# Four norms between dense stages taken in two halves of 256 tokens, with the last product unit ahead and the first one behind computed half by half

## What is computed

```python
def rms_norm(x, g): return x * rsqrt(mean(x * x, axis=-1) + EPS) * g
def modulate(h, shift, scale): return h * (1 + scale) + shift

h = modulate(rms_norm(x, norm_g), shift, scale)     # one norm ahead of every stage
x = x + 0.5 * gate * swiglu(h, w_in, w_out)         # a stage reads h and adds to x
```

## Time and profile before

| | |
|---|---|
| runs | 2886.98, 2891.97, 2892.22 us; median 2891.97 |
| profiled execution | 2890.92 us, of which the core's span is 2889.1 |
| granted TensorE clock, mean | 0.978 of full speed |
| PE (TensorE matmul) busy | 2775.0 us, 96% of the span |
| PEld (weight load) busy | 2322.7 us, 80% |
| DVE (VectorE) busy | 1519.1 us, 53% |
| ACT (ScalarE) busy | 835.0 us, 29% |
| chain that ended last | PE 93%, DVE 5%, ACT 1%, issue 1%, DMA 1% |

### The profile page before, as it was taken

One profiled execution on the slowest core, in us unless ns is written; L12 is line 12 of the kernel. 1 busy time (PEld: TensorE's weight loads), 2 busy tenths in 40 slices (PEclk: granted clock), 3 DMA queues, 4 the chain that ended last, 5 costly groups with the idle time before them and its releaser, 6 DMA issues.

```text
span 2889.1 us, 33968 instructions
## 1 busy us (share of the span) xinstructions
PE 2775.0 (96%) x13286; PEld 2322.7 (80%) x13286; DVE 1519.1 (53%) x2054; ACT 835.0 (29%) x913; POOL 75.6 (3%) x151
## 2 busy tenths in 40 slices
PE   4999998999999999999999999999999999999999
PEld 3888876888878888788788887898898878778887
DVE  6735544735556367544563455657565533354343
ACT  3212232212231122321321423345545422222221
POOL 0000000000001000000000000000000000000000
PEclk9999997999999999999999999999999999999999
DMA  7634521635526355232363332111111342222322
GB/s 272 227 130 168 196 84 67 230 117 186 176 93 235 126 170 196 88 102 98 104 228 111 128 99 92 56 37 52 45 46 43 109 153 89 87 88 87 102 90 85
DMA packets 92932, 353.43 MB, mean 122 GB/s; under 512 B 10528, under 2 KB 11296, under 8 KB 84000
## 3 DMA queue, kind: packets, MB, share of 16 engines
q1 hardware_dynamic: 73120, 250.05, 25.9%
q0 software_dynamic: 19280, 101.23, 9.6%
q10 hardware_dynamic: 432, 0.75, 0.1%
HBM read 343.60 MB, written 8.39 MB: 122 GB/s over the span
## 4 chain that ended last, share of the span: by engine, by line
PE 93%; DVE 5%; ACT 1%; issue 1%; DMA 1%; SPq 0%; DVEq 0%; ACTq 0%
PE ps L1682 24%; PE ps L1684 24%; PE ps L1683 24%; PE ps L1818 4%; PE ps L1820 4%; PE ps L1819 4%; PE ps L2060 1%; PE ps L2054 1%; PE ps L2008 1%; DVE w_raw_lo L971 1%; DVE h_lo L1107 1%; DVE ada_first L976 0%; PE ps L1767 0%; PE ps L1701 0%; PE ps L1913 0%
## 5 line engine op out<-in xcount | busy, mean ns | idle before, releaser
L1682 PE MATMUL ps<-h_hi,w_hi 128*128 128x512 f32 x2016 | 792.6, 393 | 19.6 <-DVE h_lo L1107 15.9
L1684 PE MATMUL ps<-h_hi,w_lo 128*128 128x512 f32 x2016 | 790.3, 392 | 0.0
L1683 PE MATMUL ps<-h_lo,w_hi 128*128 128x512 f32 x2016 | 790.3, 392 | 0.0
L581 ACT CAST w_hi<-w_raw 128x2048 fp32r<-128x2048 f32 (+1 forms) x240 | 422.1, 1759 | 622.6 <-PE ps L1684 537.0
L971 DVE TENSOR_TENSOR w_lo<-w_raw,w_hi 128x2048 fp32r<-128x2048 f32 (+1 forms) x219 | 458.5, 2094 | 127.8 <-ACT w_hi L581 127.3
L1682 PEld LDWEIGHTS ps<-h_hi,w_hi 128*128 128x128 f32 x2016 | 382.6, 190 | 109.1 <-issue 27.9
L1683 PEld LDWEIGHTS ps<-h_lo,w_hi 128*128 128x128 f32 x2016 | 382.8, 190 | 80.1
L1684 PEld LDWEIGHTS ps<-h_hi,w_lo 128*128 128x128 f32 x2016 | 382.0, 189 | 80.2
L1682 PE MATMUL ps<-g_hi,w_hi 128*128 128x512 f32 x960 | 373.5, 389 | 0.0
L1684 PE MATMUL ps<-g_hi,w_lo 128*128 128x512 f32 x960 | 373.4, 389 | 0.0
L1683 PE MATMUL ps<-g_lo,w_hi 128*128 128x512 f32 x960 | 373.4, 389 | 0.0
(11 more groups left out here) (292 smaller groups left out, 2761.5 us busy)
## 6 DMA issues: line engine op xcount, KB each, us to landing
w_raw<-in_units SPq DMA_DIRECT2D x350, 512.0 KB, 4.5
ada<-in_ada_t POOLq DMA_DIRECT2D x56, 1024.0 KB, 6.5
w_raw<-in_units SPq DMA_DIRECT2D x128, 352.0 KB, 3.7
ada<-in_ada_t POOLq DMA_DIRECT2D x64, 512.0 KB, 5.0
ada_first<-in_ada_t SPq DMA_DIRECT2D x8, 1024.0 KB, 18.0
x_res<-in_x SPq DMA_DIRECT2D x4, 512.0 KB, 7.8
x_home<-x_res POOLq DMA_DIRECT2D x1, 2048.0 KB, 8.5
attn_home<-attn_out POOLq DMA_DIRECT2D x8, 256.0 KB, 2.3
```

The lines of the kernel that those rows point to most:

```text
L581: nc.scalar.copy(W_HI[u.slot][:, 0:n], W_RAW[u.slot][:, 0:n]).then_inc(hi_done, 1)
L1682: pe.matmul(dst, hi[:, k, c], rhs_hi(k), start=(k == 0), stop=False)
L1683: pe.matmul(dst, hi[:, k, c], rhs_lo(k), start=False, stop=False)
L1684: last = pe.matmul(dst, lo[:, k, c], rhs_hi(k), start=False, stop=(k == kt - 1))
```

## The change

Norms 3, 4, 5 and 7 are done for tokens 0 to 255 and then for 256 to 511 (`HALF[0]`, `HALF[1]`). `LATE[r]` are the tiles of X that the last unit finishes.

- TensorE, `last_unit`: the last unit ahead is computed for the first half of the tokens, then for the second (into other PSUM banks), with matmuls of 256 columns and each weight tile loaded for each half. The one-column sums of the first half stand ahead of the last three tiles of the second half. The spread of the first half's scale stands behind the unit.
- TensorE, `first_unit`: the first unit behind is likewise two passes over its eight tiles. The second half's sums stand behind tile 1 of the first pass, its spread behind tile 6.
- VectorE and ScalarE, `norm_halves` and `first_half`: the add to X, the late squares, the root, the diagonal, and the scale, shift and low-part steps are all done on 256 columns, twice.
- The late squares are no longer added to SSQ, but summed by TensorE with one-column matmuls of their own.
- In the last unit ahead, ScalarE's early squares and VectorE's sums stand ahead of the split of the next weights where they stood behind it (VectorE for all four, ScalarE for 3 and 4).
- `split_hi(ahead)` stands between the two halves on ScalarE, `split_lo(ahead)` near the end of the second half on VectorE.
- The MLP's first quarter is written out, and the loop of three quarters is one of two; three semaphores of the convolution become one.

```diff
+        LATE = {3: (7,), 4: (7,), 5: (6, 7), 7: (6, 7)}
...
+            def norm_halves(r, g, unit, ahead):
...
+                nc.scalar.activation(RSTD4[:, 16:17], EPS_C[:], ACT.Sqrt)
+                late(0)
+                half_root(0)
+                hi(0, 0)
+                hi(0, 1)
+                late(1)
+                hi(0, 2)
+                half_root(1)
+                hi(0, 3)
...
+                hi(0, 7)
+                if ahead is not None:
+                    split_hi(at(ahead))
+                for k in range(KD):
+                    hi(1, k)
...
+            def first_half(r, u, gate):
+
+                dve.wait_ge(half_done, N_BASE[r] - r + 1)
+                for n, k in enumerate(LATE[r]):
+                    last = add_half(0, k, BANK[2 * (u % 2) + n], gate)
+                last.then_inc(half_x, 1)
...
+                diagonal(0)
+                dve.wait_ge(mod_done, g + 1)
+                scaled(0, 0)
+                scaled(0, 1)
+                lo(0, 0)
+                second_half()
+                for k in range(2, 5):
+                    scaled(0, k)
+                    lo(0, k - 1)
+                diagonal(1)
+                for k in range(5, KD):
+                    scaled(0, k)
+                    lo(0, k - 1)
+                lo(0, KD - 1)
+                scaled(1, 0)
+                for k in range(1, KD):
+                    scaled(1, k)
+                    lo(1, k - 1)
+                    if ahead is not None and k == 6:
+                        split_lo(at(ahead))
+                lo(1, KD - 1)
...
             def out_pair(j):
                 u = j + U_WO
+                if j.i is None and j.base == 3:
+                    square_sums(7, range(6))
                 split_lo(u + 1)
                 if j.i is None and j.base == 3:
-                    square_sums(7, range(6))
+                    first_half(7, u.base, 6)
+                    return
...
+            def last_unit(r, u, kt, b_hi, b_lo):
...
+                for k in range(kt):
+                    last = half_products(u, kt, tiles, own, b_hi, b_lo, 0, k)
+                last.then_inc(half_done, 1)
+                for k in range(kt):
+                    if k == kt - 3:
+                        half_sums(r, 0)
+                    last = half_products(u, kt, tiles, [BANK[4], BANK[7]], b_hi, b_lo, 1, k)
+                last.then_inc(pe_done, 1)
+                half_rows(r, 0)
+
+            def first_unit(r, u):
...
+                for k in range(KD):
+                    pe.wait_ge(h_ready, H_BASE[r] + k + 1)
+                    half_products(u, KD, 2, banks, H_HI, H_LO, 0, k)
+                    if k == 1:
+                        half_sums(r, 1)
+                    if k == 6:
+                        half_rows(r, 1)
+                for k in range(KD):
+                    pe.wait_ge(h_ready, H_BASE[r] + KD + k + 1)
+                    last = half_products(u, KD, 2, banks, H_HI, H_LO, 1, k)
+                last.then_inc(pe_done, 1)
```

More of the change, by code:

```diff
@@ L1688, in h_part, with half_sums @@
                 return lambda k: b[:, k, a:a + n]
+            def half_sums(r, h):
+                pe.wait_ge(sq_summed, S_BASE[r + 1])
+                for c in range(2):
+                    cc = slice((2 * h + c) * P, (2 * h + c + 1) * P)
+                    pe.matmul(BANK[6 + h][:, c:c + 1], SSQ[:, cc], ONES_D[:, 0:1], start=(c == 0), stop=False)
+                n = len(LATE[r])
+                pe.wait_ge(sq_made, Q_BASE[r] + KD - n + n * (h + 1))
+                for k in LATE[r]:
+                    for c in range(2):
+                        cc = slice((2 * h + c) * P, (2 * h + c + 1) * P)
+                        last = pe.matmul(BANK[6 + h][:, c:c + 1], GT[k % 2][:, cc], ONES_D[:, 0:1], start=False, stop=(k == KD - 1 and c == 1))
+                last.then_inc(ms_made, 1)
@@ new lines, in half_rows, with half_products @@
+            def half_rows(r, h):
+                pe.wait_ge(diag_made, N_BASE[r] + h + 1)
+                pe.matmul(BANK[5 - h][:, HALF[h]], ONES[:], DIAG[:, 2 * h:2 * h + 2, :].rearrange("p c t -> p (c t)"),
+                          start=True, stop=True).then_inc(rb_made, 1)
+            def half_products(u, kt, tiles, banks, b_hi, b_lo, h, k):
+                n = kt * tiles * P
+                hi = W_HI[u.slot][:, 0:n].rearrange("p (k m) -> p k m", k=kt)
+                lo = w_lo(u)[:, 0:n].rearrange("p (k m) -> p k m", k=kt)
+                for m in range(tiles):
+                    c = slice(m * P, (m + 1) * P)
+                    last = exact(banks[m][:, HALF[h]], hi[:, k, c], lo[:, k, c], b_hi[:, k, HALF[h]], b_lo[:, k, HALF[h]], k == 0, k == kt - 1)
+                return last
@@ new lines, in last_unit @@
+            def last_unit(r, u, kt, b_hi, b_lo):
+                tiles = len(LATE[r])
+                pe.wait_ge(lo_done, u.v + 1)
+                pe.wait_ge(evac_done, u.v - 1)
+                own = [BANK[2 * u.slot + m] for m in range(tiles)]
+                for k in range(kt):
[7 more added lines that the diff above has]
+                half_rows(r, 0)
@@ new lines, in first_unit @@
+            def first_unit(r, u):
+                pe.wait_ge(lo_done, u.v + 1)
+                pe.wait_ge(evac_done, u.v - 1)
+                banks = [BANK[2 * u.slot + m] for m in range(2)]
+                for k in range(KD):
[9 more added lines that the diff above has]
+                last.then_inc(pe_done, 1)
@@ L1690, in norm, with exact @@
+            def exact(dst, a_hi, a_lo, b_hi, b_lo, first, last):
+                pe.matmul(dst, a_hi, b_hi, start=first, stop=False)
+                pe.matmul(dst, a_hi, b_lo, start=False, stop=False)
+                return pe.matmul(dst, a_lo, b_hi, start=False, stop=last)
             def norm(r):
-                pe.wait_ge(sq_summed, SUMS * (r + 1))
+                pe.wait_ge(sq_summed, S_BASE[r + 1])
                 for c in range(4):
                     pe.matmul(BANK[6][:, c:c + 1], SSQ[:, c * P:(c + 1) * P], ONES_D[:, 0:1], start=(c == 0), stop=False)
-                pe.wait_ge(sq_made, KD * (r + 1))
+                pe.wait_ge(sq_made, Q_BASE[r + 1])
@@ L1707, in ffn @@
                     pe.wait_ge(lo_done, base + 1)
-                    if half == 0:
+                    if half == 0 and FFN_NORM[f] not in HALVED:
                         pe.wait_ge(h_ready, H_BASE[FFN_NORM[f]] + 1)
@@ L1712, in in_unit @@
                         ready = None
+                        if half == 0 and j.i is None and j.base == 0 and FFN_NORM[f] in HALVED:
+                            first_unit(FFN_NORM[f], j + base)
+                            return
                         if half == 0 and j.base == 0 :
@@ L1814, in _ @@
             pe.matmul(BANK[6][:], ONES[:], DIAG_2[:].rearrange("p c t -> p (c t)"), start=True, stop=True).then_inc(rb2_made, 1)
-            def exact(dst, a_hi, a_lo, b_hi, b_lo, first, last):
-                pe.matmul(dst, a_hi, b_hi, start=first, stop=False)
-                pe.matmul(dst, a_hi, b_lo, start=False, stop=False)
-                return pe.matmul(dst, a_lo, b_hi, start=False, stop=last)
             def ctx_products(u, cols, width, dst):
@@ L2192, in _ @@
             each(pe, 4, 0, 2, out_pair)
-            norm(7)
             def quarter(q):
                 for j in range(4):
-                    ready = (lambda k: pe.wait_ge(h_ready, H_BASE[7] + k + 1)) if j == 0 else None
-                    products(q.times(8) + (U_MLP + j), KD, 2, h_part(H_HI), h_part(H_LO), ready).then_inc(pe_done, 1)
+                    if j == 0 and q.i is None and q.base == 0:
+                        first_unit(7, at(U_MLP))
+                        continue
+                    products(q.times(8) + (U_MLP + j), KD, 2, h_part(H_HI), h_part(H_LO)).then_inc(pe_done, 1)
                 for j in range(4):
```

170 lines of the change are left out of this document (123 added, 47 removed).

## The result

The changed kernel took 2906.24 us in the median of 4 runs (2905.04 to 2907.67), the kernel before 2891.24 in 4 runs beside it (2886.98 to 2892.22). The ratio is 1.0054 with a 95% interval of 1.0041 to 1.0067: slower by 15 us, where 12 had been forecast. The profiled execution took 2905.04 us with a span of 2903.4.

The account below looks back on a forecast made before the run. TensorE bounds the kernel, busy 96% of the span. At full clock 3.1 us more plus 9.6 of clock falls gives 12.7 over 2890.92: 2903.6, stated as 2903; own range 2897 to 2909, 8 in 10 2889 to 2912.

Parts of the forecast that it names:

- The prices of a half: A 256-column matmul costs 0.120 us against 0.227 whole; a VectorE half step 0.395, 60% of a whole, a pair 0.79.
- Rival 2: Four norms: TensorE sets the pace if a VectorE pair is under 0.72 us; 23 us less, 2868; chance 0.06.
- Stretch A: First matmul of last unit ahead to VectorE's first scaled tile: 9.8 us (norms 3, 4), 15.5 (5, 7); 17.7 less.
- The stand of 1.6: TensorE, last unit at norms 5 and 7: waits 1.6 us for the first half's add and squares.
- Stretch B at full clock: VectorE's first scaled tile to first matmul of second unit behind: 20.65, 20.65, 21.5, 22.1 us; 20.8 more.
- The second root: ScalarE, second half's root between shifts of tiles 2 and 3: VectorE stands about 1.6 us for it.
- the second spread: Behind TensorE's tile 6 of the first pass: VectorE stands about 1.1 us before starting the second half.
- Sum at full clock: Both stretches of the four norms without clock falls: 20.8 - 17.7 = 3.1 us more.
- The clock: Falls to 1.2 GHz: 4 us each at norms 5, 7; even chance of 1.6 each at 3, 4; together 9.6.
- Doubled matmuls, 4.6 us: Four norms: 354 matmuls become 708 half ones, 84.8 us against 80.2, 4.6 more at full clock.
- Rival 1: Four norms: the halves keep TensorE busy enough, the clock holds; 2894, no measurable change; chance 0.17.
- Rival 3: The clock falls twice at each norm and stays low through the first unit; 2911; chance 0.13.

Follow-up runs that it names:

- e7: e6 plus the first half's add ahead of the weight split, the split as VectorE's last step, low parts later, norm 7's next weights inside the norm; 2878.3 us.
- e8: e7 plus six fillers (fp32r matmuls of 256 columns that keep TensorE busy) behind the second half's sums; 2875.1 us.
- e10: e8 with ScalarE's second root behind the shift of tile 1, and squares and sums of tiles 0 to 3 a unit earlier at norms 5 and 7; 2875.4 us.
- e11: e10 plus fp32r fillers ahead of the second half's sums, 4 at norms 3 and 4, 9 at norms 5 and 7; 2874.3 us.
- e5: Changed kernel plus fillers (fp32r matmuls of 256 columns where TensorE stood) at the four norms; 2892.2 us.
- e1: Changed kernel with VectorE's add of the first half ahead of the weight split at norms 5 and 7; 2898.7 us.
- e9: Kernel before (no halves) plus fp32r fillers of 512 columns where TensorE stands at the four norms; 2887.0 us.
- e6: Changed kernel with the second half's add, squares, sums, root, diagonal and spread moved earlier; 2889.3 us.

## Why the prediction was right, point by point

The forecast was 2903 us from +12.7 in the norms; they gave +12.7, and the span 1.6 more. The mechanism is borne out: the stands are where it put them, and the halves lose at full clock and again by the clock. That the sum fits to a tenth is luck: two terms missed by 2.3 us in opposite directions.

- *The prices of a half:* right. VectorE's pairs lie 0.79 us apart (837.09 for 836.30), a filler or product of 256 columns 0.12. Rival 2 wanted a pair under 0.72; it is 0.79 in every run with halves in B, and 0.91 in part of e7, e8, e10 and e11.
- *Stretch A:* 9.59 for 9.8 at norms 3 and 4. At norms 5 and 7 18.23 and 16.45, with the clock held (e5) 15.43 and 15.42 for 15.5. The stand of 1.6 was 1.72, and e1 shows its cause.
- *Stretch B at full clock:* 20.2, 20.2, 21.1 and 21.6 in e5 for 20.65, 20.65, 21.5 and 22.1: each forecast 0.4 to 0.5 too long. The second root held VectorE for 1.37 at norms 3 and 4 and not 1.6 (1.72 at norms 5 and 7), the second spread for 0.84 and not 1.1. TensorE's stand for the split was 2.0 (2.3), that for norm 7's weights 2.57 (2.7).
- *Sum at full clock:* 133.2 - 132.4 = 0.8 for 3.1. This term of the sum was mis-sized, by those small parts (0.5 us in A, 1.8 in B). The 132.4 holds the kernel before at its own clock, as the prediction says; without the 4.9 us of falls that e9 took out, the halves lose 5.7.
- *The clock:* 11.9 for 9.6. Norms 5 and 7 cost 4.5 and 3.3 for 4 each; norms 3 and 4, which I had given an even chance of 1.6, cost 2.9 and 1.2. At norms 5 and 7 the place was right, within the last unit, and at norm 3 the way in which a fall costs: the stand for the second root grew from 1.37 to 2.34 because the sums in front of it ran at 0.50 (the root came 5.5 us behind VectorE's start instead of 4.6; at norm 4, where the clock held until then, 4.6). At norms 3 and 4 there is a fall behind the stand for the weight split too, at norm 4 the only one, and the prediction had none there.
- *Doubled matmuls, 4.6 us:* only the part in A lies on the path. No run took it alone; e6 and e7, with the same 708 matmuls, show that it doesn't set B.
- *Rival 1 (the clock holds, 2894):* its condition was made in e5, and its time came out, 2892.
- *Rival 3 (two falls at each norm, 2911):* two falls came at norms 3 and 5, one at norms 4 and 7, and they cost 11.9 and not 17.

## What to carry to other kernels

Cutting a stage in halves to start earlier pays only if the consumer's work does not grow by more: here A won 18.2 us (e5 against the kernel before) and B gave back 19.0, since a half step of VectorE costs 60% of a whole and small stages of the second half stood in its way. Where each small stage of the second half stands in the queues decides the rest: put it where its engine would stand anyway, not between the steps of the engine that sets the pace; that was worth 15 us of the norms here by itself (e6, falls included) and 27 with the add and the split moved too (e7), which turned the change from slower to faster. Price a clock fall by filling the stands with matmuls of the cheap type in an otherwise unchanged kernel, and do it for both kernels: here the falls cost the changed one 11.9 us and the one before at least 4.9.
